# GpSimd makes the low part of each weight unit in four subtractions of 256 columns instead of one of 1024

## What is computed

```
h = rms_norm(x, mix_norm_g);  proj = h @ w_in            # first block
x = x + concat(fox_attention, diff_attention) @ w_out
x = x + (silu(rms_norm(x) @ w_gate) * (rms_norm(x) @ w_up)) @ w_down
z = rmsnorm(x) @ w_in_2 + b_in_2                          # second block
u = silu(layernorm(dwconv31(c_a * sigmoid(c_b))))
x = x + (sigmoid(g_a) * (na @ w_na_out) + sigmoid(g_b) * (u @ w_conv_out)) @ w_out_2
x = x + (gelu(gate) * val) @ w_down_2;  out = rmsnorm(x)
```

## Time and profile before

| | us |
|---|---|
| median of 3 runs (lowest, highest) | 1466.75 (1462.83, 1468.73) |
| the profiled execution | 1462.85 |
| its span, first to last instruction | 1460.8 |
| TensorE busy | 1401.2 |
| VectorE busy | 760.7 |
| GpSimd busy | 543.4 |

### The profile page before, as it was taken

One profiled execution on the slowest core, in us unless ns is written; L12 is line 12 of the kernel. 1 busy time (PEld: TensorE's weight loads), 2 busy tenths in 40 slices (PEclk: granted clock), 3 DMA queues, 4 the chain that ended last, 5 costly groups with the idle time before them and its releaser, 6 DMA issues. The chain is left out here.

```text
span 1460.8 us, 18829 instructions
## 1 busy us (share of the span) xinstructions
PE 1401.2 (96%) x6620; PEld 1136.0 (78%) x6620; DVE 760.7 (52%) x1229; ACT 603.2 (41%) x928; POOL 543.4 (37%) x242
## 2 busy tenths in 40 slices
PE   7999999989999999999988999978999999999998
PEld 5877887667888888888768777766788888888887
DVE  6687646565322222223368887896745555552011
ACT  5444433365543443333342554424335444443223
POOL 4321132123544444444252312443444444444441
PEclk9999999899999999999989999999999999999999
DMA  4221121012433333333642211322233333333331
GB/s 142 78 57 44 44 72 59 29 44 67 121 101 88 99 101 96 92 94 95 78 135 68 59 47 55 90 83 67 76 103 90 98 101 95 91 100 90 96 102 59
DMA packets 223630, 120.70 MB, mean 83 GB/s; under 512 B 15172, under 2 KB 222417, under 8 KB 223569
## 3 DMA queue, kind: packets, MB, share of 16 engines
q1 hardware_dynamic: 223569, 119.89, 29.1%
HBM read 117.56 MB, written 2.31 MB: 82 GB/s over the span
## 5 line engine op out<-in xcount | busy, mean ns | idle before, releaser
L517 POOL TENSOR_TENSOR WL<-RAW,WH 128x1024 fp32r<-128x1024 f32 (+1 forms) x220 | 537.7, 2447 | 885.8 <-ACT WH L1051 885.7
L642 PE MATMUL PS<-XH,WH 128*128 128x512 f32 x1088 | 435.6, 400 | 19.3 <-POOL WL L517 9.6
L644 PE MATMUL PS<-XH,WL 128*128 128x512 f32 x1088 | 424.9, 391 | 0.0
L643 PE MATMUL PS<-XL,WH 128*128 128x512 f32 x1088 | 424.4, 390 | 0.0
L1051 ACT ACTIVATE WH<-RAW 128x1024 fp32r<-128x1024 f32 (+1 forms) x220 | 228.8, 1042 | 400.1 <-PE PS L644 361.2
L642 PEld LDWEIGHTS PS<-XH,WH 128*128 128x128 f32 x1088 | 205.8, 189 | 63.9 <-POOL WL L517 10.1
L644 PEld LDWEIGHTS PS<-XH,WL 128*128 128x128 f32 x1088 | 204.6, 188 | 43.8
L643 PEld LDWEIGHTS PS<-XL,WH 128*128 128x128 f32 x1088 | 205.0, 188 | 39.8 <-issue 0.7
L642 PE MATMUL PS<-HH,WH 128*128 128x512 f32 (+1 forms) x374 | 141.0, 377 | 0.0
L643 PE MATMUL PS<-HL,WH 128*128 128x512 f32 (+1 forms) x374 | 140.8, 377 | 0.0
L644 PE MATMUL PS<-HH,WL 128*128 128x512 f32 (+1 forms) x374 | 140.8, 377 | 0.0
(11 more groups left out here) (305 smaller groups left out, 2002.5 us busy)
## 6 DMA issues: line engine op xcount, KB each, us to landing
RAW<-in_w_up SPq DMA_DIRECT2D x66, 512.0 KB, 3.8
RAW<-in_w_in SPq DMA_DIRECT2D x60, 512.0 KB, 3.8
RAW<-in_w_down SPq DMA_DIRECT2D x32, 512.0 KB, 3.9
RAW<-in_w_gate SPq DMA_DIRECT2D x22, 512.0 KB, 3.8
RAW<-in_w_out SPq DMA_DIRECT2D x16, 512.0 KB, 3.6
RAW<-in_w_down SPq DMA_DIRECT2D x16, 384.0 KB, 3.3
XTM<-in_x SPq DMA_DIRECT2D x4, 512.0 KB, 6.4
RAW<-in_w_na_out SPq DMA_DIRECT2D x4, 512.0 KB, 3.3
```

The costliest lines, as they stand in the source:

```text
L517: pool.tensor_tensor(WL[:, s, 0:width], RAW[:, s % 2, 0:width], WH[:, s, 0:width].bitcast(F32), ALU.subtract).then_inc(w_lo, 1)
L642: pe.matmul(out, ah, bh, start=start, stop=False)
L643: pe.matmul(out, ah, bl, start=False, stop=False)
L644: return pe.matmul(out, al, bh, start=False, stop=stop)
```

## The change

The subtraction of a unit is cut into pieces of 256 columns: four instructions for a unit of 1024, three for one of 768. The two waits stay ahead of the first piece. The last piece updates w_lo. No tile, load or other instruction is changed.

```diff
+LOW_PIECE = 256
...
             pool.wait_ge(w_hi, u + 1)
             if not (isinstance(n, int) and n == 0):
                 pool.wait_ge(w_used, u - 3)
-            pool.tensor_tensor(WL[:, s, 0:width], RAW[:, s % 2, 0:width], WH[:, s, 0:width].bitcast(F32),
-                               ALU.subtract).then_inc(w_lo, 1)
+            for c in range(0, width, LOW_PIECE):
+                cs = slice(c, c + LOW_PIECE)
+                ins = pool.tensor_tensor(WL[:, s, cs], RAW[:, s % 2, cs], WH[:, s, cs].bitcast(F32), ALU.subtract)
+            ins.then_inc(w_lo, 1)
```

## The result

The changed kernel takes 1447.76 us (median of 4 runs, 1440.35 to 1450.82) against 1466.2 us: a ratio of 0.9872, 95% interval 0.9845 to 0.9898, so 1.3% faster. The same kernel timed again gave 0.9898 (0.9876 to 0.9920), 15 us. The profiled execution took 1450.82 us, the slowest of its four, while the one of before is the fastest of its four; the two traces therefore differ by only 12 us.

The account below looks back on a forecast made before the run. TensorE's matmuls were taken to bound the kernel, leaving some 50 us of idle time to win or lose. Terms summed to -9.8 us, less 1.0 for hand-overs: -8.8 us, so 1458 us; range 1453 to 1472 us.

Parts of the forecast that it names:

- Rival (b): GpSimd keeps its turn over all four pieces, so a block is some 2.6 us: slower, 1477 us; chance 0.10.
- Rival (c): VectorE wins the time but TensorE doesn't, through later waits and a lower clock: +0.5 us, 1467 us; chance 0.15.
- The term of the gates: 926 to 985 us: nine units' 19.4 us of VectorE blocks become 28 blocks of 0.56 us: -3.7 us.
- A piece should hold it for 0.56 us: Every blocked VectorE instruction: a piece of 256 columns blocks it for 0.56 us, the fixed part not included.
- LSUM's two blocks: At 985.12 us: one whole unit's block of 2.1 us becomes two of 0.56 us: -1.0 us.
- "1.0 off" for hand-overs: Extra hand-overs between VectorE and GpSimd, 19 in the gates alone, cost some hundredths each: 1.0 us off the gain.
- Rival (a): Fixed part is held too, or pieces meet more contending instructions than counted: only -3.0 us, 1463.7 us; chance 0.20.
- 776 to 790 us: Convolution taps at 771 and 777.74 us: each unit's block falls from 2.1 to 1.7 us, twice: -0.8 us.
- SG: 1004 to 1017 us: two of four pieces fall beside an instruction reading PSUM, shortening TensorE's waits: -1.1 us.
- WFL: At 32.53 us: one piece replaces the whole unit in the block, and TensorE's wait goes: -1.1 us.
- QL's wait at 80.6 us: TensorE's wait behind a blocked VectorE instruction of 2.9 us goes; priced with KL at 145.59 us, together -1.3 us.
- The added GpSimd time: At 737 us, where load, copy and subtraction follow each other with TensorE idle: +0.5 us on the path.

Follow-up runs that it names:

- gates_only: Pieces of 256 columns for units 128 to 139 alone, whole units for the 208 others, against the kernel before: ratio 0.9947 (0.9930 to 0.9964).
- mid_only: Pieces of 256 columns for units 100 to 151 alone, whole units elsewhere, against the kernel before: ratio 0.9930 (0.9904 to 0.9956).
- rest_only: Pieces of 256 columns everywhere but in units 100 to 151, which stay whole, against the kernel before: ratio 0.9990 (0.9970 to 1.0010).
- the hybrid: The changed kernel with pieces of 128 columns for units 128 to 135, 256 for all others: 1446.4 us, ratio 0.9868 (0.9838 to 0.9899).
- mix_after: The changed kernel with four weight loads (units 104 to 107) spread among the 16 bias transfers: 1449.87 us, ratio 0.9886 (0.9856 to 0.9916).
- the two pairs with moved loads: Kernel before and changed kernel, weight loads moved: two ahead of the bias transfers, 0.9998 and 0.9902; four spread among them, 0.9980 and 0.9886.

## Why the prediction was too small

**The mechanism was right.** VectorE and GpSimd take turns instruction by instruction, pieces beside an instruction that reads PSUM are free, and TensorE's time moves where VectorE sets it. Rival (b), a turn kept over four pieces, is out: rows of 1.22 us, one per piece. The page "SBUF — State Buffer" of the Trainium skill, in "Who interferes with whom", says that the shared port is held for the whole instruction and the other engine blocks fully; the trace agrees but for some 0.26 us: the blocks of 2.14 and 0.48 us stand beside GpSimd instructions of 2.41 and 0.74 us (medians). Rival (c) is out: in gates_only a gain of 6.7 us in the trace goes with 7.8 us of measured time, so it reaches the end.

**The term of the gates was mis-sized.** "A piece should hold it for 0.56 us" is the step: it was drawn from the slope between two widths of GpSimd's duration, 558 ns for 256 columns. The block measures 0.48 us for most taps and 0.49 on average. The count of 28 blocks for nine units is exactly what the trace has. It was right in the sum alone: the prediction put three into each of seven tiles and seven into one, and the trace has three in two tiles and two, four or five in the other six. That the errors cancel is luck. The 28 blocks make 13.7 us and not 15.7, for 19.3: -5.6. LSUM's two blocks measured 0.47 and 0.41 us where 0.56 each was put, 0.9 us for 2.1: -1.2. That gives -6.8 us, what the stretch shows, where -4.7 was put. My own row had part of it: 2.14 us for 1024 columns leaves 0.53 us at most for a quarter, which would have made 0.7 us of the 2. The further "1.0 off" for hand-overs had no row, and no such cost shows: each block is 0.07 us less than its columns. Perhaps VectorE's instruction has begun before it must wait; no run shows why. Rival (a), which put 176 ns on top of each piece, falls by the same rows. The figure of "GPSIMD Engine Reference" of the Trainium skill, section 7, 102 cycles per read command, stands there for kernels that issue many small read commands. A block four times as frequent showed no such part. The duration of a subtraction does have 170 ns that don't depend on its width, which agree in size; how many read commands it issues no run shows.

**Two stretches had too little or no term.** From 790 to 830 us two whole units back to back blocked SQ and PR (L1705) at the start of the attention by 1.2 and 1.5 us; I had looked at waits of TensorE over 0.4 us only, and there they are shorter and more (-1.0 to -1.3 us in every trace with pieces of 256 or 512 there). At 776 to 790 us I put -0.8 us; the blocks gave 1.0 us (mid_only) and the clock, for which the prediction had no term, up to 1.5 more. SG gave 1.8 us for 1.1. The clock has a part here too: the stretch at half clock behind the wait for LSUM is 6.8 us long in the kernel before and 3.4 in both traces of the changed one, and in mid_only, where it is 6.8 again, SG's stretch gained 1.4.

**The first 100 us.** Both terms came, nearly as put. Between 25 and 40 us of before TensorE gains 1.5 us or more for WFL (1.1 was put) in all traces with pieces of 256 there. At 46 us 0.9 us of it are lost in a new wait for T (L1504): three small VectorE instructions in front of it take 0.68 to 0.75 us where they took 0.16 to 0.23, so VectorE comes there only 0.6 us earlier. QL's wait at 80.6 us gives 0.9 to 1.0 us in each of these traces (0.8 was put). Together that is -1.6 us for -1.9. The table's first row hides it, because a stretch at half clock near 70 us comes and goes: it is 3.4 us long in the changed kernel, 6.8 in its repeat, and 3.4 in the repeat of the kernel before, with whole units. The three traces with pieces of 256 from the start and no such stretch (rest_only, the hybrid and mix_after) are 1.7 to 2.0 us ahead at 100 us. The added GpSimd time (0.5 us at 737 us) can't be told under a wait that varies between 8.5 and 15.3 us.

**The sum.** What comes back is -1.6 (first 100 us), -0.6 (KL), -2.5 (taps), -1.1 (790 to 926), -6.8 (gates, LSUM), -1.85 (SG) and -1.25 (T at L1984), -15.7 us. The timings say 18 (15 to 23), 15 (12 to 18) and, in the two pairs with moved loads, 14 each, so the steps account for the gain. Of the 7 us between the forecast of -8.8 and -15.7, the gates with LSUM are 2.1, the taps 1.7, nearly all of it clock, the stretch without a term 1.1, the hand-overs 1.0, SG 0.7 and GpSimd's +0.5 at the wait for WL; the first 100 us take back 0.3. The first measurement lay 2 to 3 us further out than this sum, within its interval. The range's low end stood 5 us beyond the forecast: it allowed for costs that were not there and for none of the gains that had no term.

## What to carry to other kernels

Where an engine's instructions show two durations for the same shape, look for the instruction of the other engine beside the long one; for VectorE and GpSimd the loss is close to the length of what the other is doing. Here it paid to cut long GpSimd instructions until GpSimd itself was nearly late, and not further. It pays where VectorE sets the time: 12 of 220 units brought half the gain here, and 168 others nothing measurable. Price a block from blocked rows (blocked minus unblocked, per column), not from the blocker's own duration. And before a visible wait is removed, ask which engine is the next bound in the same stretch: here 9.6 us of waiting were worth 0.2%.

## What the runs showed of the hardware

A blocked VectorE instruction is longer by 2.15 ns per column of the GpSimd subtraction beside it, less 0.07 us: 2.14, 1.04, 0.48, 0.21 and 0.08 us for 1024, 512, 256, 128 and 64 columns. A cut adds nothing to a block, but each piece can block another instruction. It does cost GpSimd time: the shortest subtraction takes 716 ns for 256 columns and 443 ns for 128 (2.13 ns per column and 170 ns fixed), of which some 42 ns overlap with the next one when they follow each other directly. GpSimd's busy time for the low parts, its own waits for VectorE included, goes from 537.7 us with whole units to 680.2 with pieces of 256 and 828.7 with pieces of 128. And after a wait of TensorE of the same length the clock may be full in one kernel and half in another (781 to 787 us: 1.00 and 0.72 after waits of 2.5 and 2.6 us), which moves up to 1.5 us without a change in any instruction of that stretch.
